# Hybrid decoder step on one core: the last fixed expert pair summed by slot matmuls, the norm row spread earlier, the overflow loop moved

## The reference, cut to what matters

```
x = x + merged @ w_out
p_group = softmax(h @ w_rg + b_rg);  g_star = argmax(p_group)          # 4 groups
top_v, top_i = top_k(expert logits of group g_star, 2)                  # 8 experts in a group
w_top = softmax(top_v) * p_group[g_star]
out = sum over the two chosen experts e:  w * (silu(h @ w_eg[e]) * (h @ w_eu[e])) @ w_ed[e]
x = x + out
y = rmsnorm(x) * norm_final
```

## Time and profile before

| | |
|---|---|
| median of 3 runs | 798.0 us (797.69 to 798.62) |
| the profiled execution's own time | 798.78 us |
| its span | 796.7 us |
| PE, DVE, ACT, POOL busy | 715.7, 340.8, 246.0, 82.2 us |
| moved by DMA | 172.49 MB, mean 216 GB/s |

### The profile page before, as it was taken

How to read it: one execution, slowest core, us unless ns; L and a number is a source line. 1 busy time by engine, 2 the same in 40 slices (tenths; PEclk the granted TensorE clock), 3 DMA queues, 4 the chain that set the end, 5 groups by cost and what they waited for, 6 DMA issues and landing times.

```text
span 796.7 us, 12378 instructions
## 1 busy us (share of the span) xinstructions
PE 715.7 (90%) x5118; PEld 534.2 (67%) x5118; DVE 340.8 (43%) x630; ACT 246.0 (31%) x496; POOL 82.2 (10%) x135
## 2 busy tenths in 40 slices
PE   4999999999999999999999999989999977777730
PEld 3888997778999999778999977864444422222210
DVE  6653359654565336435344532751323211111128
ACT  6233474544454342334222232411111100100013
POOL 2404000000000100000000010221113121111100
PEclk9999999999999999999999999989999999999985
DMA  8732111113132722613223289889999999999945
GB/s 314 230 107 62 54 53 53 54 53 106 54 98 62 264 82 99 220 53 97 62 80 110 78 297 398 302 284 374 419 415 418 418 418 417 419 419 419 412 163 219
DMA packets 82503, 172.49 MB, mean 216 GB/s; under 512 B 8064, under 2 KB 42208, under 8 KB 82432
## 3 DMA queue, kind: packets, MB, share of 16 engines
q1 hardware_dynamic: 72736, 148.51, 50.2%
q0 software_dynamic: 9712, 23.20, 7.9%
HBM read 162.73 MB, written 18.74 MB: 228 GB/s over the span
## 4 chain that ended last, share of the span: by engine, by line
PE 69%; SPq 14%; DVE 8%; DMA 4%; ACT 3%; issue 2%; POOLq 0%; ACTq 0%; DVEq 0%
PE bank L756 44%; SPq L566 10%; PE bank L1219 7%; PE bank L1235 4%; SPq L572 3%; DMA expert_down<-in_w_exp_down 2%; DVE w_split L1593 2%; PE bank L1151 1%; ACT w_split L1273 1%; PE bank L776 1%; PE bank L1186 1%; PE bank L1041 1%; PE bank L1047 1%; DMA x_rows<-in_x_prompt 1%; DVE token_out L2185 1%
## 5 line engine op out<-in xcount | busy, mean ns | idle before, releaser
L756 PE MATMUL bank<-hT_split,w_split 128*128 128x272 f32 x1152 | 154.1, 292 | 0.0
L756 PEld LDWEIGHTS bank<-hT_split,w_split 128*128 128x128 f32 x1152 | 147.4, 188 | 2.1 <-issue 0.9
L1219 PE MATMUL bank<-expert_gate_up,gatheredT 128*64 128x512 f32 x512 | 115.0, 595 | 21.3 <-DMA expert_gate_up<-in_w_exp_up 20.4
L756 PE MATMUL bank<-w_split,hT_split 128*128 128x512 f32 (+1 forms) x576 | 130.9, 381 | 0.4 <-DVE w_split L1593 0.4
L756 PEld LDWEIGHTS bank<-w_split,hT_split 128*128 128x128 f32 x576 | 100.6, 189 | 23.1 <-issue 3.3
L1593 DVE TENSOR_TENSOR w_split<-w_raw,w_split 128x2048 fp32r<-128x2048 f32 (+1 forms) x35 | 75.9, 2168 | 83.7 <-ACT w_split L1273 83.7
L1219 PEld LDWEIGHTS bank<-expert_gate_up,gatheredT 128*64 128x64 f32 x512 | 39.4, 137 | 93.7 <-issue 62.8
L1273 ACT ACTIVATE w_split<-w_raw 128x2048 fp32r<-128x2048 f32 (+1 forms) x35 | 63.4, 1812 | 42.4 <-PE bank L756 17.5
L1235 PE MATMUL bank<-expert_down,expert_actT 128*64 128x512 f32 x256 | 58.5, 597 | 13.2 <-DMA expert_down<-in_w_exp_down 8.1
L2156 DVE TENSOR_TENSOR expert_act<-expert_silu,bank 128x256 f32<-128x256 f32 x16 | 6.7, 421 | 119.5 <-ACT expert_silu L1547 119.5
L756 PE MATMUL bank<-gla_outT_split,w_split 128*128 128x272 f32 x384 | 49.4, 288 | 0.0
(11 more groups left out here) (372 smaller groups left out, 837.0 us busy)
## 6 DMA issues: line engine op xcount, KB each, us to landing
expert_gate_up<-in_w_exp_gate SPq DMA_DIRECT2D x64, 512.0 KB, 14.4
expert_gate_up<-in_w_exp_up SPq DMA_DIRECT2D x64, 512.0 KB, 15.3
expert_down<-in_w_exp_down SPq DMA_DIRECT2D x32, 1024.0 KB, 17.2
w_raw<-in_w_in SPq DMA_DIRECT2D x15, 1024.0 KB, 5.5
w_raw<-in_w_in SPq DMA_DIRECT2D x16, 512.0 KB, 4.7
s_state<-in_state_gla POOLq DMA_DIRECT2D x4, 1024.0 KB, 9.5
out_sample_gla_state<-s_state POOLq DMA_DIRECT2D x4, 1024.0 KB, 6.1
w_raw<-in_w_proj_gla SPq DMA_DIRECT2D x8, 512.0 KB, 4.4
```

The lines of the kernel that those rows point to most:

```text
L756: ins = mm(out, stat(x, k), mov(y, k), start=first and n == 0 and m == 0, stop=last and n == len(ks) - 1 and m == 2)
L1219: ins = mm(P[2 + u][64 * half:64 * half + 64, :].rearrange("p (m n) -> p m n", m=2), XT[0][:, k, 64 * half:64 * half + 64], WGU[gb][:, k / ...
```

## The change

1. **Last pair.** Pair 15 is no longer scattered. Its rows stay in `expert_out`. DVE makes a matrix `SPREAD_LAST` (128 slots x 544 tokens) that has a token's weight where the slot holds that token; PE multiplies it with `expert_out`, block by block, into PSUM, and the sum goes from there into the token's row. The weights per slot come from a small table of three bf16 digits, which PE makes behind pair 1. For blocks 0 to 2 PE adds the second expert's rows too, with a diagonal matrix of the weights (`DIAG2`); for block 3 DVE does it as before; block 4 is summed whole on PE (`ST4`). The scratch tensor is filled with zeros early in the mixer, by one POOL transfer of 1088 rows of 4 KB, since pair 15's rows in it are no longer written.
2. **Read back.** SP queues the ten reads of the scratch tensor behind the last weights, when pair 14's scatter has landed.
3. **Overflow loop.** Pairs 12 and 13 and any overflow pairs run in the loop; pairs 14 and 15 come behind it. Before, the loop held 14, 15 and the overflow.
4. **Norm row.** The two matmuls that spread `norm_final`, and the ACT copies behind them, stand ahead of the counting instead of behind the tables. `keep_clock` is 6 ahead of them and 4 behind (13 before), and 6 behind the tables (5 before, beside the two row matmuls).
5. On DVE the order of the end is written out by hand; ten small operations for the weights are added in the router and eight for the matrices ahead of pair 14.

The diff, cut to its core:

```
-PEELED = NFIX // 2 - 1
+PEELED = NFIX // 2 - 2
+SEQ = NFIX - 2
+BY_PE = (0, 1, 2)
...
@@ block.sync
+            for kh in range(2):
+                sp.wait_ge(gu_done, 4 * looped + (4 * PEELED - 3 + kh))
+                load_gate_up(0, pair(SEQ + 1), kh)
+            sp.wait_ge(dn_done, 2 * looped + (2 * PEELED - 1))
+            load_down(0, pair(SEQ + 1))
-            sp.wait_ge(scattered[0], 16 * turns)
-            sp.wait_ge(scattered[1], 16 * turns)
+            sp.wait_ge(scattered[0], 16 * turns + 16)
             for bl in range(NB):
                 for k in range(2):
+                    dst = YI[2 * bl + k][:] if bl < 4 else X2[32 + 32 * k:64 + 32 * k, 4, :]
...
@@ block.gpsimd
+            pool.dma_start(tok_d.rearrange("(p r) (c n) -> p (r c) n", p=16, c=2),
+                           WF2[16:32, :].unsqueeze(1).to_broadcast([16, 2 * NTOK * 2 // 16, 512])).then_inc(zeros_stored, 16)
             pool.wait_ge(s_made, 2)
...
+            move_rows(turns, 0, last=True)
...
@@ block.tensor
-            keep_clock(13)
+            keep_clock(6)
+            pe.wait_ge(memset_done, 2)
+            pe.wait_ge(nfin_in, 16)
+            for c in range(2):
+                ins = mm(P[2 + c][:], ONEROW[:], NFIN[0:1, 512 * c:512 * c + 512], start=True, stop=True)
+            ins.then_inc(nfin_mm, 1)
+            keep_clock(4)
             pe.wait_ge(sel_ready, 1)
...
             pe.wait_ge(lg_out, NB)
-            pe.wait_ge(nfin_in, 16)
-            for c in range(2):
-                ins = mm(P[2 + c][:], ONEROW[:], NFIN[0:1, 512 * c:512 * c + 512], start=True, stop=True)
-            ins.then_inc(nfin_mm, 1)
-            keep_clock(5)
+            keep_clock(6)
             pe.wait_ge(gathered[0], 16)
             turn_rows(0)
...
+            for bl in range(NB):
...
+                if bl in BY_PE or bl == 4:
+                    pe.wait_ge(x_in[bl], 16 + 32)
+                    for c in range(2):
+                        half = slice(512 * c, 512 * c + 512)
+                        if bl == 4:
+                            mm(banks[c], ST4[0:96, :], X2[0:96, 4, half], start=True, stop=False)
+                        else:
+                            mm(banks[c], DIAG2[bl][:], YI[2 * bl + 1][:, half], start=True, stop=False)
+                if bl == 0:
+                    pe.wait_ge(y_out_a, 2 * turns + 3)
+                    pe.wait_ge(y_out_v, 2 * turns + 3)
+                for c in range(2):
+                    ins = mm(banks[c], SPREAD_LAST[:, cols], YO[:, 512 * c:512 * c + 512], start=bl not in BY_PE and bl < 4, stop=True)
+                ins.then_inc(sums_mm, 1)
...
@@ block.vector
+            def banks_sum(bl):
+                y1 = two_halves(YI[2 * bl][:])
+                dve.wait_ge(dve_step, added[bl])
+                dve.wait_ge(sums_mm, bl + 1)
+                V.tensor_tensor(y1, BANKS[:, 2 * bl:2 * bl + 2, :], y1, ALU.add).then_inc(x3_ready, 1)
...
```

More of the change, by code:

```diff
@@ L1221, in expert_pair @@
                 ins.then_inc(gu_done, 1)
-                pe.wait_ge(gathered[v], 16 * i + (16 if u == 0 else 32))
-                turn_rows(v)
+                if not (last and u):
+                    pe.wait_ge(gathered[v], 16 * i + (16 if u == 0 else 32))
+                    turn_rows(v)
                 pe.wait_ge(act_done, n + 2)
@@ L1526, in _ @@
             run_units(range(NU))
+            act.wait_ge(nfin_mm, 1)
+            A(NFIN[:, 0:512], P[2][:], ACT.Copy)
+            A(NFIN[:, 512:D], P[3][:], ACT.Copy).then_inc(nfin_out, 1)
             act.wait_ge(exp_in, 2)
@@ L1547, in expert_pair @@
                 A(SA[:], P[2 + u][:, 0:FF], ACT.Silu).then_inc(silu_done, 1)
-                act.wait_ge(xg_turned, n + 3)
-                xt_half()
+                if not (last and u):
+                    act.wait_ge(xg_turned, n + 3)
+                    xt_half()
                 act.wait_ge(dn_done, n + 1)
@@ L1562, in _ @@
                     expert_pair(i, u)
+            for u in range(2):
+                expert_pair(turns, u, last=True)
             A(DUMMY[:], EPSC[:], ACT.Sqrt)
             for bl in range(NB):
-                act.wait_ge(x3_ready, bl + 1)
+                n = rows(bl)
+                if bl < 4:
+                    act.wait_ge(x3_ready, bl + 1)
+                else:
+                    act.wait_ge(sums_mm, NB)
                 act.wait_ge(squares, 3 * NB + bl)
-                A(JUNK3[0:rows(bl), :], YI[2 * bl][0:rows(bl), :], ACT.Square, accum_out=SSQ[0:rows(bl), bl:bl + 1]).then_inc(squares, 1)
+                A(two_halves(JUNK3[0:n, :]), two_halves(YI[2 * bl][:]) if bl < 4 else BANKS[0:n, 0:2, :], ACT.Square,
+                  accum_out=SSQ[0:n, bl:bl + 1]).then_inc(squares, 1)
                 act.wait_ge(squares, 3 * NB + bl + 1)
@@ L2175, in _ @@
                     expert_pair(i, u)
[L2177 to L2181, removed]
-                dve.wait_ge(x_in[bl], 16 + 32)
[L2183 to L2186, removed]
+            link(V.memset(IONES[:], 1.0))
@@ new lines, in _, with first_expert @@
+            dve.wait_ge(w4_in, 32)
+            for p0, p1, q in ((0, 64, 0), (64, 96, 64)):
+                ins = V.scalar_tensor_tensor(out=ST4[p0:p1, :], in0=same[p0:p1, q:q + 32], scalar=W4[p0:p1, :],
+                                             in1=same[p0:p1, q:q + 32], op0=ALU.mult, op1=ALU.mult)
+            ins.then_inc(spread_ready, 1)
+            added = {}
+            def first_expert(bl):
+                y1 = YI[2 * bl][:]
+                dve.wait_ge(x_in[bl], 16 + 32)
+                chain[0] += 1
+                added[bl] = chain[0]
+                V.scalar_tensor_tensor(out=y1, in0=y1, scalar=R1["w1"][:, bl:bl + 1], in1=X2[:, bl, :],
+                                       op0=ALU.mult, op1=ALU.add).then_inc(dve_step, 1)
```

168 lines of the change are left out of this document (130 added, 38 removed).

## The result

| | before | after |
|---|---|---|
| median of 5 runs | 798.0 us (796.78 to 798.84) | 805.0 us (803.11 to 806.75) |
| the profiled execution's own time, span | 798.78, 796.7 us | 806.75, 804.6 us |
| last down weights landed | 761.3 us | 778.5 us |
| from there to the span's end | 35.4 us | 26.1 us |

The change makes the kernel slower by 0.9% (ratio 1.0088, 95% interval 1.0064 to 1.0112). The forecast was 798.4 us, in a range of 792.0 to 803.0: the time lies above it.

A forecast was written before the change was run, and what follows sets the result against it. From 550 us to the last weights the DMA engines were taken to set the pace, so delays before and the chain after count. End -8.9 plus router +9.3 gave +0.4 us: 798.4 us, in a range of 792.0 to 803.0.

The forecast's parts named there:

- What costs nothing: Zero fill, small DVE operations, matrices, index copies and moved loop were called hidden behind waits or DMA-paced work: 0 us.
- The cover that I named: In the mixer, the weight unit queued at 70.33 us was said to be read by ACT 9.9 us later.
- my upper bound of 6: In the mixer, a weight unit wholly behind the zero fill would be 6 us late.
- The router: PE waits for the norm row, clock halves, counting starts 11.1 us later; full DMA stretch starts 9.3 us later.
- The rival in which PE waits less: In the router, PE is held but loses less: full stretch 5.9 us late, 795.0 us; chance 0.16.
- the slower rival: After the router, the second gather takes 6.8 us, SP's down weights come 12.7 us late: 801.8 us; chance 0.24.
- The end: After the last weights, dropping the scatter and the wait for the read gains 8.9 us.
- of DVE's own length only a little is gained: At the end, DVE has five products instead of ten, but four sums out of PSUM come in.
- The sum: Whole kernel: end -8.9 plus router +9.3 gives +0.4 us.

The follow-up runs named there:

- x1: The kernel before with only the zero fill added, from the change's 16 partitions and at its place: 805.2 us, 1.0096 of before.
- x4: The changed kernel with the zero fill read from a tile of 128 partitions: 798.0 us, 1.0011 of before.
- y4: The kernel before plus a zero fill from 16 partitions that lie 8 apart, same pieces: 798.1 us, 1.0001 of before.
- x2: The kernel before with only the norm-row matmuls, their copies and the fillers moved as in the change: 808.8 us, 1.014 of before.
- y3: y1, but SP queues the ten reads only when the last pair's expert_out is written: 794.8 us, 0.9965 of before.
- z2: y1, with the second expert's rows of blocks 0 to 2 added by DVE instead of PE: 790.5 us, 0.9914 of before.
- y2: x4 with the norm-row matmuls, copies and fillers put back as in the kernel before: 787.0 us, 0.9867 of before.
- y1: x4 with the norm row loaded early in the mixer, its matmuls still ahead of the counting: 787.3 us, 0.9881 of before.
- z1: x2 with 22 fillers instead of 6 ahead of PE's wait for the norm row: 805.1 us, 1.0098 of before.

## Why the prediction was wrong

**The step that failed** is "What costs nothing. The zero fill: 4.46 MB, 10.7 us at full rate ... I take 0." The term is +6.4 in the trace and +7.5 by x1's median. What was mis-sized is the fill's own time, 48.7 us where I had 10.7. The rate came from the expert stretch, where each transfer reaches all 128 partitions; none of my rows showed a transfer out of 16 neighbouring partitions, so full speed was an assumption and should have been one end of the range.

The cover that I named was misread too. `w_raw` has two buffers, and SP queues a unit when the unit two before it has been split: the unit queued at 70.33 is not the one that ACT splits at 80.18 but the next, at 95.83. Its cover is 25.5 us, not 9.9; that of the unit queued at 84.44 and split at 114.31 is 29.9. The first was hardly held up (5.3 us in after, 6.2 in x4). The second takes 5.5 us beside x4's fill and 14.1 beside y4's, which 29.9 hides, and 35.9 in after, which it does not. With the true cover even a unit wholly behind a fill of 10.7 us would have cost nothing. So my upper bound of 6 was near the truth by luck, from a fill far too short and a cover far too small; and it had neither a rival nor a chance.

The Trainium skill has the rule that I did not weigh: "SBUF — State Buffer", section "Door 1: The DMA port swizzle", says that a transfer's speed depends on how many of the 16 SBUF ports its partitions reach. By its mapping partitions 16 to 31 reach 4 of them, every 8th partition 8, and a full tile all. Of the section's 435 GB/s that would be 109 and 218 (estimates); the runs show 98 to 101 (after) and 204 GB/s (y4), in the same ratio, and 421 in x4 from 75 to 85 us, near the full rate. So the traces agree with the rule.

**The router** was right in its mechanism and short by 1.5 us (9.3 forecast, 10.8 measured; in the traces of x2 and x4 the term is 10.6 and 9.8). PE waits for the row, the load takes 9.4 us, the clock is halved, row matmuls and fillers take twice as long: each nearly as forecast. The counting starts 11.8 us later, the 6.4 taken off, for a forecast of 11.1. What I took wrongly is that from there to the second gather nothing changes: it took 7.1 us before (528.82 - 521.71) and takes 8.95 now (548.83 - 539.88), since the five fillers behind the counting run at half clock too (4.15 us). The gather itself took 4.0 us where I had 3.4. The rival in which PE waits less did not occur; the slower rival had the right size (12.7 at the gather, 12.4 measured) for another reason, and SP's gate weights were late by less, 10.6.

**The end** was right: -9.3 against -8.9, matmuls, sums and first product within 0.1 us of their forecasts. y3 and z2 show what carries it: with late reads only 2.2 of it are left, without PE's diagonal matmuls 2.7 less. I had written that of DVE's own length only a little is gained; z2 shows that the diagonal matmuls are worth about 3 us, because they pay for the four sums that come in.

**The sum** itself: 6.4 + 10.8 - 9.3 = +7.9, the difference of the spans. With the fill at the 0 that I took, x4 gives 798.0 us, where 798.4 were forecast. The other terms that I took at nothing, the moved loop and the small DVE operations, are in y2 as well; it is faster than before by more than the end's 9.3, so they show no cost. Two equal and opposite large terms leave the sign to what was taken as nothing.

## What to carry to other kernels

Read a DMA's speed off the partitions that it touches, not off its bytes: a fill out of 16 neighbouring partitions ran at a quarter of the speed, and a weight unit on another queue took 36 us beside it. A small load that PE waits for belongs far ahead of its use: queued in the mixer (y1) it cost nothing; queued behind the store and asked for at once, it cost 11 us (x2). When you look for what covers a transfer, follow the buffer: which use waits for this load, and not which use comes next. Price each new transfer from a row of its own kind, and where there is none, let "it is hidden" be a rival with a chance.

## What the runs showed of the hardware

- The same 4.46 MB out of SBUF took 48.7 us from 16 neighbouring partitions (98 to 101 GB/s), 25.4 us from 16 partitions that lie 8 apart (204 GB/s), and 15.8 us from all 128 (421 GB/s from 75 to 85 us).
- The slow fill held the engines for the other queue too: of the 1 MiB that SP queued at 84.64 no packet moved up to 90 us, its queue had 0.6% of the 16 engines' time to 100 us, and it took 35.9 us in all; queued at the same place beside y4's fill, twice as fast, it took 14.1, and 4.9 in before.
- A 4 KB load behind a 512 KB store in POOL's queue, beside full weight traffic, took 8.4 to 9.7 us in all nine kernels of this case that have it there. The same 4 KB took 2.8 to 3.6 us near 262 us in the three that load them early (y1, y3, z2), where in y1 the engines moved under 140 GB/s in the 2.5 us behind the issue. Whether the store or the weights make the difference is not separated.
- PE's clock is a cost of a wait beyond its length: in after a stop of 7.3 us was followed by 20 us at 0.50 to 0.68, and keeping PE busy with useless matmuls through the same wait gave back 3.6 us (z1).
